# Order of the expert groups in the first layer: context group alternately last and first, rows turned in pairs

## The reference

```python
def expert_choice_ffn(h, w_router, w_gate, w_up, w_down):
    ...
    cap = CAPACITY_FACTOR * n // N_EXPERTS
    ...
    gates, idx = lax.top_k(affinity, cap)
    xs = jax.vmap(lambda hb, ib: hb[ib])(h, idx)
    a = jnp.einsum('becd,edf->becf', xs, w_gate)
    u = jnp.einsum('becd,edf->becf', xs, w_up)
    y = jnp.einsum('becf,efd->becd', jax.nn.silu(a) * u, w_down) * gates[..., None].astype(h.dtype)
```

## Time and profile before

| | |
|---|---|
| median of three runs | 2151.52 us (2147.84 to 2155.16) |
| the profiled execution | 2153.24 us, of which the span of the trace 2151.4 |
| TensorE busy in the span | 1967.2 us (91%) |
| VectorE, ScalarE, POOL busy | 663.7, 530.3, 156.7 us |
| first layer's expert stages, 645 to 1188 us | TensorE busy 538.1 of 543.0, DMA 400 GB/s |
| TensorE's waits for weights there | 4.9 us in six waits |
| second layer's expert stages, 1800 to 2100 us | TensorE busy 81 to 84 of each 100, DMA 427 GB/s |

### The profile page before, as it was taken

How to read it: one execution, slowest core, us unless ns; L and a number is a source line. 1 busy time by engine, 2 the same in 40 slices (tenths; PEclk the granted TensorE clock), 3 DMA queues, 4 the chain that set the end, 5 groups by cost and what they waited for, 6 DMA issues and landing times. The chain is left out here.

```text
span 2151.4 us, 27244 instructions
## 1 busy us (share of the span) xinstructions
PE 1967.2 (91%) x10872; PEld 929.0 (43%) x10872; DVE 663.7 (31%) x1746; ACT 530.3 (25%) x1222; POOL 156.7 (7%) x155
## 2 busy tenths in 40 slices
PE   5999989999979999999999899889996898888875
PEld 2436455555642332323323556455554333333322
DVE  3322345666540100101001632366665011020203
ACT  3211154565531000100100421165553110000001
POOL 1100010000010010020100101100001000000000
PEclk9999979999989999999999999999998899999999
DMA  9742020000189999999999302020008899999995
GB/s 353 282 168 81 0 79 1 1 2 1 40 336 410 422 363 418 379 391 418 364 414 422 146 20 79 19 61 1 1 1 333 368 427 427 427 426 427 427 426 227
DMA packets 90935, 515.66 MB, mean 240 GB/s; under 512 B 10594, under 2 KB 15628, under 8 KB 36540
## 3 DMA queue, kind: packets, MB, share of 16 engines
q1 hardware_dynamic: 84496, 493.29, 56.6%
q0 software_dynamic: 4416, 15.21, 2.3%
q10 hardware_dynamic: 1900, 5.43, 0.6%
HBM read 498.69 MB, written 15.20 MB: 239 GB/s over the span
## 5 line engine op out<-in xcount | busy, mean ns | idle before, releaser
L732 PE MATMUL psS<-arena 128*64 128x512 f32 (+9 forms) x4552 | 1135.7, 556 | 71.7 <-DMA arena<-in_w_up 25.4
L732 PEld LDWEIGHTS psS<-arena 128*64 128x64 f32 (+4 forms) x4552 | 449.6, 158 | 667.2 <-issue 585.4
L1952 DVE TENSOR_REDUCE mx<-psS 128x1 f32<-128x768 f32 (+2 forms) x200 | 165.5, 827 | 151.1 <-PE psS L732 149.5
L1298 ACT ACTIVATE arena<-psT 128x768 f32<-128x768 f32 (+7 forms) x261 | 150.3, 577 | 243.3 <-PE psT L735 229.6
L735 PE MATMUL psT<-ident,arena 128*128 128x128 f32 (+1 forms) x1036 | 172.1, 290 | 35.6 <-ACT arena L1298 9.1
L1298 ACT ACTIVATE arena<-psS 128x128 f32<-128x128 f32 (+5 forms) x158 | 61.8, 421 | 573.3 <-PE psS L732 528.6
L2136 DVE TENSOR_TENSOR arena<-arena,psS 128x512 f32<-128x512 f32 x32 | 20.6, 684 | 551.6 <-PE psS L732 551.6
L735 PEld LDWEIGHTS psT<-ident,arena 128*128 128x128 f32 (+1 forms) x1036 | 119.9, 144 | 134.7 <-issue 96.7
L732 PE MATMUL psT<-arena 128*32 128x512 f32 x1536 | 174.5, 595 | 0.0
L1298 ACT ACTIVATE arena<-psS,nb 128x768 f32<-128x768 f32 (+2 forms) x200 | 158.1, 794 | 1.4
L732 PE MATMUL psM<-arena 128*128 128x512 f32 x288 | 140.1, 608 | 0.0
(11 more groups left out here) (226 smaller groups left out, 1264.7 us busy)
## 6 DMA issues: line engine op xcount, KB each, us to landing
arena<-in_w_gate SPq DMA_DIRECT2D x117, 1024.0 KB, 12.4
arena<-in_w_up SPq DMA_DIRECT2D x116, 1024.0 KB, 18.3
arena<-in_w_down SPq DMA_DIRECT2D x116, 1024.0 KB, 17.7
arena<-in_w_mod SPq DMA_DIRECT2D x48, 1024.0 KB, 7.5
arena<-in_w_in SPq DMA_DIRECT2D x6, 2048.0 KB, 7.8
arena<-in_w_out SPq DMA_DIRECT2D x8, 512.0 KB, 7.9
arena<-in_w_out SPq DMA_DIRECT2D x2, 2048.0 KB, 15.4
normed_rows<-arena ACTq DMA_DIRECT2D x8, 512.0 KB, 7.9
```

What stands on the lines that cost most here:

```text
L732: return nc.tensor.matmul(o, lhsT, rhs, start=start, stop=stop)
L1298: return nc.scalar.activation(o, i, f, **kw)
L1952: link(V.reduce_max(mx[:, par:par + 1], view(S, 0, P, 0, (512, 2), (1, n)), axis=AX.XY))
```

## The change

In the first layer the order of the groups in a stage now comes from a table: L0 L1 C or C L0 L1, in turn, so that two C groups or two pairs of latent groups adjoin over the border of two stages, save between stages 7 and 8 and from stage 11 to the next quad's stage 0. A group that comes first in its stage waits for the loads of its experts, so C waits for all four where it is first. Hidden tiles are turned in the order 2, 0, 1, and the next quad's rows two tiles at a time at four places instead of one tile at eight. ScalarE takes the silus, and VectorE the products and copies, in the order 2, 0, 1. What waits on a count of finished groups now counts by the place of the group in its stage. Nothing is computed that was not computed before, and no load, no slot and no buffer is changed.

```diff
-TURN_AT = {(8, 1): (0,), (8, 2): (1,), (9, 0): (2,), (9, 1): (3,), (9, 2): (4,), (10, 0): (5,), (10, 1): (6,), (10, 2): (7,)}
+CLL, LLC = (2, 0, 1), (0, 1, 2)
+HIDDEN_AT = {(7, 0): 2, (7, 1): 0, (8, 2): 1}
+STAGE_ORDER = (LLC, CLL, LLC, CLL, LLC, CLL, LLC, CLL, CLL, LLC, CLL, LLC)
+TURN_AT = {(8, 1): (0, 1), (9, 1): (2, 3), (10, 2): (4, 5), (11, 1): (6, 7)}
...
+        def order(l, q, st):
+
+            if l:
+                return (0, 1)
+            return (2, 0, 1) if q * NSTAGE + st == NQ * NSTAGE - 1 else STAGE_ORDER[st % NSTAGE]
+
         def groups_done(l, q, st, g):
 
-            return l * NQ * NSTAGE * (SW[0] // P) + (q * NSTAGE + st) * (SW[l] // P) + g + 1
+            return l * NQ * NSTAGE * (SW[0] // P) + (q * NSTAGE + st) * (SW[l] // P) + order(l, q, st).index(g) + 1
+
+        def stage_done(l, q, st):
+            return groups_done(l, q, st, order(l, q, st)[-1])
...
+        def hidden_order(l):
+            return (2, 0, 1) if l == 0 else (0, 1)
+
+        def hidden_turn(l, q, g):
+            return hidden_tile(l, q, hidden_order(l).index(g))
...
-                        sp.wait_ge(z["done"], groups_done(l, 0, st, 2 if l == 0 else e // 2))
+                        sp.wait_ge(z["done"], groups_done(l, 0, st, e // 2) if l else stage_done(l, 0, st))
...
-                        for e in experts if (q, st) == (NQ - 1, NSTAGE - 1) else ():
+                        for e in experts if order(l, q, st)[0] == g else ():
                             pe.wait_ge(*slot_filled(l, (q * NSTAGE + st) * QUAD + e))
...
-                        for g in last_order(l) if (q, st) == (NQ - 1, NSTAGE - 1) else range(NX):
-                            if st == 8 and g == 1 and wc:
-                                turn_hidden(q, 2)
+                        for g in (last_order(l) if not wc and (q, st) == (NQ - 1, NSTAGE - 1) else order(l, q, st)):
                             group(q, st, g)
-                            if st == 7 and g == 1:
+                            if wc and (st, g) in HIDDEN_AT:
+                                turn_hidden(q, HIDDEN_AT[st, g])
+                            if not wc and st == 7 and g == 1:
                                 turn_hidden(q, 0)
-                            if st == 7 and g == NX - 1:
                                 turn_hidden(q, 1)
...
-                    for g in range(NX):
+                    for g in hidden_order(l):
                         act.wait_ge(z["done"], groups_done(l, q, 3, g))
...
+                    if wc:
+                        gated(q, 2)
                     gated(q, 0)
+                    if wc:
+                        hidden(q, 2)
                     gated(q, 1)
                     hidden(q, 0)
-                    if wc:
-                        gated(q, 2)
                     hidden(q, 1)
-                    if wc:
-                        hidden(q, 2)
```

More of the change, by code:

```diff
@@ L466, in exchanged_through, with hidden_tile @@
             return 2 * ((l * TT + i) * 3 + n + 1)
-        def hidden_tile(l, q, g):
-            return l * NQ * (SW[0] // P) + q * (SW[l] // P) + g + 1
+        def hidden_tile(l, q, n):
+            return l * NQ * (SW[0] // P) + q * (SW[l] // P) + n + 1
+        def hidden_order(l):
+            return (2, 0, 1) if l == 0 else (0, 1)
+        def hidden_turn(l, q, g):
+            return hidden_tile(l, q, hidden_order(l).index(g))
         def last_group(l, q, g):
@@ L570, in _ @@
                     up_projections()
-                    sp.wait_ge(z["done"], groups_done(l - 1, NQ - 1, 7, 2))
+                    sp.wait_ge(z["done"], stage_done(l - 1, NQ - 1, 7))
                     section_rows(0, 0, WIN_EARLY)
@@ L1194, in turn_hidden @@
                 def turn_hidden(q, g):
-                    pe.wait_ge(z["prod"], hidden_tile(l, q, g))
+                    pe.wait_ge(z["prod"], hidden_turn(l, q, g))
                     for b in range(2):
@@ L1201, in turn_hidden @@
                         last.then_inc(z["hp"], 1)
-                        free[6 + b] = (z["he"], 2 * hidden_tile(l, q, g) - 1 + b)
+                        free[6 + b] = (z["he"], 2 * hidden_turn(l, q, g) - 1 + b)
                 last_late = range((MOD_FRONT + 1) * KD, len(MOD_CHUNKS))
@@ L1239, in group @@
                         pe.wait_ge(z["ge"], KD * (q + 1) - 4)
-                    elif q == 0 and m == 0 and g == 0:
+                    elif q == 0 and m == 0 and g == order(l, q, st)[0]:
                         pe.wait_ge(z["ge"], kq + 1)
@@ L1243, in group @@
                     elif st == 4:
-                        pe.wait_ge(z["silu"], hidden_tile(l, q, g))
+                        pe.wait_ge(z["silu"], hidden_turn(l, q, g))
                     elif st == 8:
-                        pe.wait_ge(z["he"], 2 * hidden_tile(l, q, g))
+                        pe.wait_ge(z["he"], 2 * hidden_turn(l, q, g))
                     if g < 2:
@@ L2132, in gated @@
                     dve.wait_ge(z["done"], groups_done(l, q, 7, g))
-                    dve.wait_ge(z["silu"], hidden_tile(l, q, g))
+                    dve.wait_ge(z["silu"], hidden_turn(l, q, g))
                     for h in range(2):
@@ L2140, in hidden @@
                     for b in range(2):
-                        dve.wait_ge(z["hp"], 2 * hidden_tile(l, q, g) - 1 + b)
+                        dve.wait_ge(z["hp"], 2 * hidden_turn(l, q, g) - 1 + b)
                         V.tensor_copy(view(ar, 0, P, HIDT + 4 * b * W + g * P, (W, 4), (1, P)),
@@ L2145, in weighted @@
                 def weighted(q, g):
-                    dve.wait_ge(z["done"], groups_done(l, q, 11, last_group(l, q, g)))
+                    dve.wait_ge(z["done"], groups_done(l, q, 11, g))
                     c = q + 8 if g == 2 else q * 2 + g
```

## The result

The changed kernel took 2156.69 us (median of 8 runs, 2152.29 to 2163.82) against 2151.44 of the kernel before beside it: ratio 1.0029, 95% interval 1.0019 to 1.0039. The profiled execution took 2159.39 us with a span of 2157.6, 6.2 more than before.

A forecast was written before the change was run, and what follows sets the result against it. TensorE and DMA were both taken as nearly full, with weight landings limiting each quad's middle. 5.0 us of lateness, net of saved runs, plus 3 us of clock falls on 2151.52 gave 2159.5 us, range 2148 to 2165.

The forecast's parts named there:

- The runs: First layer's expert stages: fewer unbroken runs of one tile shape on TensorE save their fixed parts, 8.4 us in all.
- The lateness: Context-first stages in each quad's middle wait for their fourth load; carried on, the layer ends 5.0 us later.
- the landing moves with the quad's start: Quads after the first begin with a full ring, so load landings shift with the quad's start; quad 1 carries 1.11 us.
- a faster TensorE doesn't bring this landing forward: Quad 0, stage 7: DMA is already at full rate, so the fourth load lands at 723.7, making the stage 2.47 us late.
- The clock: TensorE's clock halves behind the longer waits before context-first groups: three falls of 1 us each, 3 us in all.
- The sign asked for: In the changed kernel's timeline, granted clock of 0.50 for some 3 us behind at least two of the waits.
- The row of 2.25: Profile row before the change: a TensorE wait of 2.25 us followed by clock 0.50 for the next 3 us.
- The sum: Whole kernel: 5.0 us late plus 3 us of clock falls, 8.0 us added to 2151.52, giving 2159.5 us.
- rival (a): Clock stays high behind the stages' waits, so only the 5.0 us of lateness counts: 2156.5 us; chance 0.22.
- What hides the rest: ScalarE's paired row turns cost TensorE nothing; scatter-adds are in before the context silu, else stage 4 is held 2 to 3 us.
- Rival (b): Loads have more room, fourth loads of stages 5 and 7 land 2.5 to 3.5 us earlier, 8.4 us saved: 2143.1; chance 0.13.

The follow-up runs named there:

- kernels with half loads: Kernel before and changed kernel, each bringing only half of every first-layer weight load from quad 0's third stage on: ratios 0.9979 and 0.9948 to the kernel before.
- second trace: The changed kernel, nothing altered, run and traced once more beside the kernel before: 2158.43 us against 2150.34, ratio 1.0035, stages 549.05 us.
- first trace: The changed kernel's first profiled execution, beside the kernel before: 2159.39 us, stages 548.4; median of its runs 2156.69 us, ratio 1.0029.

## Why the prediction was right, and where it was not

**The runs.** Right: 8.23 us without the loads' limit against 8.4. Against the kernels with half loads, whole loads cost the kernel before 6.2 us (543.0 less 536.8) and the changed one 19.8 (548.4 less 528.6): 13.6 more, of which the shorter runs give back 8.2.

**The lateness.** Right in place and nearly in size: 5.0 us worked out, 5.4 measured without a fall of the clock, and 4.4 in the second trace, once its fall of 1.7 is taken off. That the first sum comes so near is in part luck: quad 0 lost 0.9 us less than worked out and quad 3 1.2 more. By quad, longer than before:

| quad | worked out | first trace | second trace |
|---|---|---|---|
| 0 | 1.1 | 0.2 | 1.7, with a fall of the clock of 1.7 |
| 1 | 0.8 | 1.0 | 1.1 |
| 2 | 0.9 | 0.8 | 0.8 |
| 3 | 2.3 | 3.5 | 2.4 |

For quads 1 and 2 the rule "the landing moves with the quad's start" held to 0.2 us: C of stage 5 starts 56.06 and 56.17 us after its quad, and the landings of before lay at 55.9 and 56.2 (less the starts 782.5 and 918.5). For quad 0 the step "a faster TensorE doesn't bring this landing forward" was off by 1 us: 77.8 instead of 78.7. For quad 3, where the rule should hold too, it moved later, by 1.2 in the first trace and 0.1 in the second; why stays open.

**The clock.** This is the step that failed in the first trace: three falls of 1 us each, and there was none behind 2.36 to 2.60 us. The sign asked for, 0.50 behind at least two of the waits, came in neither trace. The row of 2.25 was taken for a threshold. Over the traces of all kernels here with whole loads, in the expert stages of the first layer, the clock fell behind none of 52 waits under 2.0 us, behind 8 of 19 from 2.18 to 2.60, and behind 6 of 8 from 2.90 to 5.46. A fall behind 2.2 to 2.6 us made the work behind it 1.5 to 1.7 us longer, not 1, but the stages only where the next group's weights were there: in three of the eight the slower work took the place of a wait of 1.2 us of the next group (stage 6 of quad 3, argued from the traces without a fall), and 0 to 0.2 us were lost. Length alone does not decide it: 2.18 us, twice in one trace, gave both. For the changed kernel that is 0 and 1.7 us in two traces with four such waits each, where the sum had 3. A chance for each fall would have been the right form of the term. The Trainium skill ("TensorE: Matmul & The Clock Gate", section "Why this matters for your kernels") warns of idle gaps, but of longer ones than these 2.2 to 2.6 us. The first trace agrees with it; seven others do not, with falls behind 2.18, 2.19, 2.25, 2.37, 2.51, 2.56, 2.57 and 2.58 us.

**The sum.** By the mechanism that the traces show, the first comparison (5.2 us) was rival (a), whose 2156.5 was closest. The second (8.1 us) is the forecast's 8.0 in size only: its trace holds 4.4 of lateness and 1.7 of the clock, and the other 2 us are not in its stages; the rest of the span differs by up to 5 us from trace to trace.

**What hides the rest.** Right for the adds and ScalarE: in the changed kernel no group waits for a silu. That this hangs on stage 3 being context first, I had not seen; put back, it costs 2.2 us in each quad.

**Rival (b), all 8.4 us.** It fell: the fourth loads came 77.8 us after the start of quad 0 and 56.1 and 56.2 after those of quads 1 and 2, at most 0.9 us sooner than before, where it asked for 2.5 to 3.5. The DMA's mean share doesn't say how much room there was. A stretch in which the DMA is full reads 1.01 or 1.02 (the windows above), so the 0.99 of the earlier trace rows, like the 1.00 with pairs of rows, is a mean of full stretches and of pauses at the ends of quads (0.78). With pairs of rows, and with stage 9 or stages 1 and 9 context first besides, the stages took 538.4 to 540.1 us. Whether an order with whole loads can go below that, no run here shows.

## What to carry to other kernels

Where two engines both read 0.99 over a stretch, the mean doesn't tell which of them a saving meets. Look for the parts of the stretch in which each is full. Then compare, for each group that is moved ahead in its stage, the landing of its last load with its new start, quad by quad, and carry the lateness on. Here this gave the stages at which the loss appears, and its size to 0.6 us, though single quads were off by 1; with stages 1 to 8 context first it gave 10 us for 8.7, and with stage 5 put back it missed by 3.6 and 4.7, falls of the clock included. Joining equal tile shapes was worth 0.155 us a run here (8.23 us for 53 runs), and is best placed where loads have slack.

## What the runs showed of the hardware that was not expected

The granted clock behind an idle stretch of TensorE of 2.2 to 2.6 us is not settled by that length: 1.00 eleven times and about 0.5 for 3 us eight times, among equal waits in one execution. None of 52 waits under 2.0 us lost it. That two groups which wait a little each are safer than one that waits for both is argued from these counts; no run splits one wait and changes nothing else.

What a fall costs isn't settled by its length either. Where the next group has its weights, the end moves by the full 1.7 us (C of stage 7 in the changed kernel). Where the next group would have waited, the slower work fills that wait: L0 and L1 of stage 6 in quad 3 took 8.47 to 8.72 us to the C behind them with a fall in three traces, and 8.48 without one.
